# Moving the last quarter of the memory projection from behind the first output projection into the cross attention

## What is computed

```
mixed = concatenate([att, rec]) @ w_out
x = x + rmsnorm(mixed, post_mix_g)
h = rmsnorm(x, pre_x_g)
m = rmsnorm(mem, mem_norm_g)
q = (h @ w_xq)                    # 4 heads of 256
k, v = split(m @ w_xkv)           # w_xkv is 1024 x 2048
p = softmax(q k^T / 16)           # per head, 256 x 256
x = x + rmsnorm((p v) @ w_xo, post_x_g)
h = rmsnorm(x, pre_ffn_g)         # and a gated feed-forward part follows
```

## Time and profile before

| | us |
|---|---|
| median of three runs | 1029.43 |
| lowest and highest | 1029.34, 1029.95 |
| profiled execution, its own time | 1032.41 |
| span of the profiled execution | 1030.5 |
| PE busy | 923.6 |
| DVE busy | 605.0 |
| ACT busy | 488.3 |
| POOL busy | 174.9 |

### The profile page before, as it was taken

One profiled execution on the slowest core, in us unless ns is written; L12 is line 12 of the kernel. 1 busy time (PEld: TensorE's weight loads), 2 busy tenths in 40 slices (PEclk: granted clock), 3 DMA queues, 4 the chain that ended last, 5 costly groups with the idle time before them and its releaser, 6 DMA issues.

```text
span 1030.5 us, 14724 instructions
## 1 busy us (share of the span) xinstructions
PE 923.6 (90%) x5670; PEld 823.5 (80%) x5670; DVE 605.0 (59%) x904; ACT 488.3 (47%) x815; POOL 174.9 (17%) x151
## 2 busy tenths in 40 slices
PE   4978889899886999999969999987888979999996
PEld 3966788578865999999868787877776779999996
DVE  3667865557435767676766744465456455555554
ACT  4653334446425555554454345564454364444432
POOL 2025603000000000000013336751514000000000
PEclk9999989999988999999989999999999989999999
DMA  9532422245205565655236462343224265556541
GB/s 282 194 110 95 163 83 83 82 144 181 105 1 184 204 202 169 201 171 196 102 99 223 164 238 84 127 148 144 82 82 163 71 211 189 190 177 197 172 160 41
DMA packets 93038, 152.37 MB, mean 148 GB/s; under 512 B 2133, under 2 KB 52555, under 8 KB 92731
## 3 DMA queue, kind: packets, MB, share of 16 engines
q1 hardware_dynamic: 92493, 151.04, 43.3%
q0 software_dynamic: 256, 0.26, 0.4%
q10 hardware_dynamic: 238, 0.37, 0.1%
HBM read 150.61 MB, written 1.05 MB: 147 GB/s over the span
## 4 chain that ended last, share of the span: by engine, by line
PE 78%; DVE 9%; ACT 5%; issue 3%; POOL 2%; DMA 2%; SPq 0%; DVEq 0%; POOLq 0%; ACTq 0%
PE ps L491 68%; PE ps L729 2%; DMA sb_ring<-in_w_in 2%; PE ps L572 2%; ACT sb_whi L1292 2%; PE ps L705 1%; DVE sb_wlo L1734 1%; PE ps L630 1%; DVE sb_probs L1982 1%; POOL sb_st L1154 1%; ACT sb_b L1390 1%; ACT sb_probs L1466 1%; ACT sb_b L1314 1%; DVE sb_tahi L1777 1%; DVE sb_talo L1778 1%
## 5 line engine op out<-in xcount | busy, mean ns | idle before, releaser
L2065 DVE TENSOR_TENSOR sb_wlo<-sb_ring,sb_whi 128x1024 fp32r<-128x1024 f32 x132 | 161.3, 1223 | 131.5 <-ACT sb_whi L1527 131.4
L1292 ACT ACTIVATE sb_whi<-sb_ring 128x1024 fp32r<-128x1024 f32 (+2 forms) x147 | 152.3, 1043 | 139.3 <-PE ps L491 133.0
L1734 DVE TENSOR_TENSOR sb_wlo<-sb_ring,sb_whi 128x1024 fp32r<-128x1024 f32 (+3 forms) x113 | 143.5, 1278 | 125.0 <-ACT sb_whi L1292 124.6
L1527 ACT ACTIVATE sb_whi<-sb_ring 128x1024 fp32r<-128x1024 f32 x132 | 139.5, 1058 | 149.0 <-PE ps L491 146.6
L491 PE MATMUL ps<-sb_whi,sb_tbhi 128*128 128x512 f32 (+2 forms) x376 | 147.8, 393 | 1.8 <-DVE sb_b L2035 1.0
L491 PE MATMUL ps<-sb_wlo,sb_tbhi 128*128 128x512 f32 (+2 forms) x376 | 145.4, 387 | 0.0
L491 PE MATMUL ps<-sb_whi,sb_tblo 128*128 128x512 f32 (+2 forms) x376 | 145.3, 386 | 0.0
L491 PE MATMUL ps<-sb_tahi,sb_whi 128*128 128x256 f32 x488 | 140.7, 288 | 4.3 <-DVE sb_wlo L1734 3.0
L491 PE MATMUL ps<-sb_talo,sb_whi 128*128 128x256 f32 x488 | 139.7, 286 | 0.0
L491 PE MATMUL ps<-sb_tahi,sb_wlo 128*128 128x256 f32 x488 | 139.5, 286 | 0.0
L491 PE MATMUL ps<-sb_tbhi,sb_whi 128*128 128x256 f32 x480 | 137.2, 286 | 0.6 <-DVE sb_tblo L1757 0.6
(11 more groups left out here) (196 smaller groups left out, 1471.9 us busy)
## 6 DMA issues: line engine op xcount, KB each, us to landing
sb_ring<-in_w_in SPq DMA_DIRECT2D x15, 2048.0 KB, 7.9
sb_ring<-in_w_up SPq DMA_DIRECT2D x22, 1024.0 KB, 5.1
sb_ring<-in_w_down SPq DMA_DIRECT2D x11, 1024.0 KB, 4.9
sb_ring<-in_w_ffn_gate SPq DMA_DIRECT2D x11, 1024.0 KB, 5.4
sb_ring<-in_w_ffn_up SPq DMA_DIRECT2D x11, 1024.0 KB, 5.3
sb_ring<-in_w_ffn_down SPq DMA_DIRECT2D x11, 1024.0 KB, 4.9
sb_ring<-in_w_xkv SPq DMA_DIRECT2D x4, 2048.0 KB, 8.1
sb_ring<-in_w_out SPq DMA_DIRECT2D x2, 2048.0 KB, 8.3
```

The lines of the kernel that those rows point to most:

```text
L1292: act.activation(piece_pair(m)[0], src, ACT.Copy).then_inc(s("hi_done"), 1)
L1527: act.activation(*ffn_half_io(f, c, what, part, 0), ACT.Copy).then_inc(s(f"ffn{f}_hi"), 1)
L1734: dve.tensor_tensor(low, pieces[m][1], high.bitcast(F32), ALU.subtract).then_inc(s("lo_dve"), 1)
L2065: dve.tensor_tensor(low, raw, high.bitcast(F32), ALU.subtract).then_inc(s(f"ffn{f}_lo"), 1)
```

## The change

`xkv3` leaves its place behind w_out in PE's queue. It becomes the `fill` of the cross attention: its first half in step 0, its second in step 1. Its weights are loaded behind w_xq instead of ahead of it. Its results are taken out of PSUM by ACT in steps 2 and 3 of `attend`, and PE waits for them before the values of head 2. Since `memT` must live until then, `hTx` gets another place: the pair `TC`, laid over the buffers `b1` and `b6`, which are unused at that time. The pieces that ACT and DVE split ahead are renumbered to fit.

```diff
@@ buffers
-        B = [sb(f"b{i}", [P, R * D]) for i in range(10)]
+        B, B_AT = [], []
+        for i in range(10):
+            B.append(sb(f"b{i}", [P, R * D]))
+            B_AT.append(nc.sbuf_base - 4 * R * D)
+        TC = [nc.alloc_sbuf_tensor_at(f"tc{part}", [P, KT * S], F32R, offset=B_AT[i]) for i, part in ((1, "hi"), (6, "lo"))]
...
-        hT1, memT, mixT, hTx, oxT, hTf1 = pair(TA), pair(TB), pair(TA), pair(TB), pair(TA), pair(TB)
+        hT1, memT, mixT, hTx, oxT, hTf1 = pair(TA), pair(TB), pair(TA), pair(TC), pair(TA), pair(TB)
@@ order of the loads
-            if n == "w_out":
+            if n == "w_xq":
                 chunk("xkv3", a["w_xkv"], KT, 512 * 3, 512)
@@ TensorE
-            gemm_rows("xkv3", memT)
-
             turn_norm("pre_x_g")
...
-                        pe.wait_ge(*banks.empty(f"xkv{2 + c}.{half}"))
+                for r in range(R):
+                    pe.wait_ge(*banks.empty(f"xkv2.{r}"))
...
             def valuesx(h, o, pT):
+                if h == X_HEADS // 2:
+                    for r in range(R):
+                        pe.wait_ge(*banks.empty(f"xkv3.{r}"))
...
-            attend("attx", X_HEADS, readyx, by_rows(scoresx, (S, S)), valuesx, (S, S))
+            attend("attx", X_HEADS, readyx, by_rows(scoresx, (S, S)), valuesx, (S, S),
+                   fill=[(gemm_rows, ("xkv3", memT, 0)), (gemm_rows, ("xkv3", memT, 1))])
@@ ScalarE
-            post_rows("w_out", lambda: ahead_of("xkv3", 2))
-            pre_norm("pre_x_g", x, [], hTx, gain_at("pre_x_g"), lambda: ahead_of("w_xq0", 1),
-                     added="w_out_added", before=lambda: ahead_of("xkv3", 4), after=lambda: ahead_of("w_xq0", 2))
-            for r in range(R):
-                take_rows(f"xkv3.{r}", xv[:, r, 512:1024])
+            post_rows("w_out")
+            pre_norm("pre_x_g", x, [], hTx, gain_at("pre_x_g"), lambda: ahead_of("w_xq0", 3),
+                     added="w_out_added", before=lambda: ahead_of("w_xq0", 2))
...
-            attend("attx", X_HEADS, (S, S))
+            attend("attx", X_HEADS, (S, S),
+                   fill=[(lambda: None, ())] * 2 + [(take_rows, (f"xkv3.{r}", xv[:, r, 512:1024])) for r in range(R)])
@@ VectorE
-            ahead_of("xkv3", 2)
             residual("w_out", quarters("w_out"), 1)
             pre_norm("pre_x_g", x, hTx, gain_at("pre_x_g"),
-                     lambda: ahead_of("xkv3", 4), lambda: ahead_of("w_xq0", 2))
-            ahead_of("w_xo0", 3)
+                     lambda: ahead_of("w_xq0", 1), lambda: ahead_of("w_xq0", 3))
+            ahead_of("xkv3", 1)
```

## The result

| | before | changed |
|---|---|---|
| median, us | 1029.38 | 1038.57 |
| lowest and highest | 1029.16, 1029.95 | 1036.88, 1041.81 |
| runs | 4 | 4 |
| profiled execution, own time | 1032.41 | 1037.74 |
| its span | 1030.5 | 1035.8 |

The change makes the kernel slower: the ratio is 1.0092, with an interval of 1.0066 to 1.0118; the medians are 9.2 us apart. A second comparison (5 runs of the changed kernel, 18 of the one before) gives 1.0076 with 1.0063 to 1.0090, which is 7.8 us of 1031.10; its medians are 7.1 us apart. The forecast was +7.55 and a time of 1037.0.

A forecast was written before the change was run, and what follows sets the result against it. PE, carrying 78% of the chain that ended last, was taken to bound the kernel. The terms -2.91 + 10.98 - 0.52 = +7.55 us, on a median of 1029.43, gave 1037.0, with a range of 1034.0 to 1039.5.

The forecast's parts named there:

- rival 2: Cross attention: softmax queues behind the xkv3 splits, PE waits 2.0 us for one head, 4.0 for two: 1039.0 to 1041.0; chance 0.14.
- A: From w_out's last matmul to w_xq's first: without the cover it goes from 14.56 to 11.65 us, -2.91.
- B: Cross attention, w_xq's last matmul to w_xo's first: 10.98 us of matmuls added, 0.52 of waiting covered, +10.46 us.
- Half rate behind A: At w_xq's start: half rate taken to end with the transposes; reaching into w_xq, it would leave -1.3 of the gain.
- rival 1: Cross attention: one or both half-rate stretches are spared, 1035.4 without the first, 1033.1 without either; chance 0.20.
- rows 7: Cross attention, profile before: PE at half rate 3.20 us from 273.4 and 4.60 from 290.6; the forecast left both.
- ACT and DVE: Cross attention: xkv3's splits and copies fit among the softmax steps, 1.6 and 1.5 us free for heads 0 and 1; cost 0.
- Transfers: Weight loads: xkv3 issued at 249.2, landing at 257.5, with 3.5 us to spare; all fit, cost 0.
- Rival 3: Cross attention: the fill takes up all 10.9 us idle and slow, leaving only A's gain, 1026.6; chance 0.03.
- The clock rule: PE: half rate is default, lifted by sustained activity, back after idling; a fill might hold B at full rate, 1033.1.

The follow-up runs named there:

- experiment 7: Changed kernel with xkv3 split into two chunks of 256 columns, the first left behind w_out, the second as fill of steps 0 and 1: 1031.23 us, ratio 1.0003.
- experiment 1: The changed kernel run again with no edit: 1038.20 us, ratio 1.0076 to the kernel before.
- experiment 2: The kernel before run again with no edit, for a second profile: profiled execution 1033.61 us, span 1031.7.
- experiments 3: Changed kernel without xkv3, heads 2 and 3 using the values of heads 0 and 1: 1030.64 us, ratio 0.9995 to the kernel before.
- experiment 5: Kernel before with 48 idle matmuls of xkv3's shape added in steps 0 and 1 of the cross attention: 1041.42 us, ratio 1.0116.
- 11: Changed kernel with two pieces of w_xo0 as fill in steps 3 and 4 of the cross attention: 1034.36 us, ratio 1.0026 to the kernel before.

## Why the prediction was right

It said 1037.0 with 1034.0 to 1039.5, slower with 0.92; measured were 1038.57, and +9.2 us (medians) and +7.8 us (ratio) in the two comparisons against +7.55. The time lies 0.4 us above the band of 1036.0 to 1038.2 that the forecast itself held, towards rival 2, whose waits aren't there. The waits and the work came out as reckoned; the half rate did not, once in either direction, and that these two misses, 0.5 to 0.9 us more behind A and up to 2.8 less in B, left the sum so close is in part luck.

- **A, forecast -2.91.** The difference is 14.56 - 11.64 = 2.92. The pause is 8.31 (forecast from the place behind w_xo: 8.32), the transposes 3.67 (3.67), the stretch 11.64 (11.65). A place in the same trace with the same chain and no cover was a good measure, and experiment 7 shows that the cover is the reason.
- **Half rate behind A.** The forecast let it end with the transposes, and kept -1.3 as an end in case it reached into w_xq. It did: w_xq took 24.34 us where it had taken 23.42, so 0.92 of the 2.92 went back; in the other execution of the changed kernel it took 23.96, and 0.54 went back.
- **B, forecast +10.46.** The work is 5.46 + 5.48 = 10.94 us of chain, the wait of 0.52 is gone, the waits of 2.2, 0.5, 2.2 and 1.6 stayed. By waits and work the term holds to 0.1 us. The stretch grew by only 35.53 - 27.86 = 7.67, and was forecast at about 38. The rest of 2.8 is half rate: of the two slow stretches of the earlier trace rows, which the forecast kept, this profile has the first only, and the other execution of the changed kernel the second only (experiment 1). That is rival 1 in part. But the kernel before varies in the same way: the execution of experiment 2 lacks the late one, and against its 25.90 B grew by 9.6. To take rows 7 as a fixed property of the kernel was the mis-sized term: the profile that I read had 2.0 us more of slow work in B than the next one of the same kernel.
- **ACT and DVE, forecast 0** with 1.6 and 1.5 us free. No wait stands before the transposes of heads 0 and 1, and 1.3 us are free in both. The chain for head 0 took 5.9 us (5.8 reckoned); PE was there sooner, since its scores took 1.73 and not 1.89. Rival 2 didn't happen, and it was a closer thing than the reckoning said.
- **Transfers, forecast 0.** The load of xkv3 was issued at 248.79 against 249.2 reckoned (w_out had ended 1.3 us earlier in this execution, so that it came some 0.9 us late, about what w_xq lost at half rate); no wait for a weight piece stands in B.
- **Rival 3** (B takes up the work) falls by experiments 3, 5 and 11.

The one place where an expectation failed is the kernel without xkv3: 1026.5 forecast, 1030.64 and 1030.79 measured. The local sum was right (61.63 and 61.85, B 26.1 and 26.2) and the time was not, by some 4 us: 1.7 because the kernel before took 1031.10 in that comparison and not 1029.4, and 2.4 beyond that. About as much, 1.9 to 2.6 us, stands in the second block, where the clock was lower with no more waiting. Why, no run shows.

**The clock rule.** Behind the pause of 8.31 us PE worked at half rate, through the transposes and the first 2.3 us of w_xq, before full rate came back, which agrees with what the Trainium skill (TensorE: Matmul & The Clock Gate, Part 1: The HAM clock gate) says of sustained activity. The hope that by this rule a fill would hold B at full rate isn't borne out: with the fill the first score took 3.54 us at 0.50 in one execution and 1.97 in the other, which had its slow stretch late, and B was 35.5 us both times; experiment 5, with as much work in the same places, had both slow stretches (3.19 us for the first score, 3.30 for the values of head 2).

## What to carry to other kernels

A filler is worth the pause that it covers, and only up to that pause's end: ask which wait stands behind the place where you put it, not how much idle time the stage has in all. Half of this filler could leave its 8.3 us pause at little cost (0.2 us by the medians, some 1.5 without the help of ACT's order), the other half cost its whole length. Short waits inside an attention are better filled by pieces of the next product whose operands are ready, which costs no other place its cover: 3.9 us gained here, against 7.8 lost.

## What was not expected of the hardware

- The time of one and the same kernel is not as firm as its first three runs (1029.34 to 1029.95) made it look. In the three comparisons of the experiments the kernel before took 1027.32 to 1032.59 (18 runs), 1029.05 to 1034.56 (25 runs) and 1029.19 to 1034.53 (18 runs). Two profiles with equal waits differ in when the granted clock falls to 0.50 and for how long, and that alone is 2.0 us in 28 of stretch B.
- Behind one and the same pause of 2.21 us, with the same instructions on both sides, the first score took 3.54 us in one execution of the changed kernel and 1.97 in the next. Which pause of B is paid for a second time, in half rate, differs from execution to execution.
- Both kernels without the 48 matmuls in the first block had a lower clock in the second (0.93 over 700 to 800 against 0.96 and 0.97). Their second block also works on other values, and no run tells which of the two matters. This stays open.
